# Experts' outputs summed by token in PSUM, second matrices by column halves, two more places for weights

## The chip, the core and the metric

The kernel runs on one core of a Trainium2 chip. The metric is the device time of one execution in microseconds (us); lower is better.

## The reference, cut to what matters

Two transformer blocks over 256 tokens of width 1024, all in fp32. The change is in the end of the second: a residual of cross-attention, a mixture of 32 experts with two chosen per token, and a last norm.

```python
h = rms_norm_2(x, xattn_norm_g[l])
m = rms_norm_2(mem, mem_norm_g[l])
x = x + memory_cross_attention(h, m, w_xq[l], w_xk[l], w_xv[l], w_xo[l])
h = rms_norm_2(x, moe_norm_g[l])
x = x + hierarchical_moe(h, w_group[l], b_group[l], w_router[l], b_router[l], w1[l], w3[l], w2[l])
return rms_norm_2(x, final_norm_g)

def expert_block(args):
    xb, e = args
    return (jax.nn.silu(xb @ w1[e]) * (xb @ w3[e])) @ w2[e]
```

Each expert has `w1` and `w3` of 1024x512 and `w2` of 512x1024, 2 MB each: 192 MB in all, every byte of which is read.

## The kernel before

**Layout.** The state is kept by feature: X2 is 128 partitions x 8 feature blocks x 256 tokens, the lower half of each 512-wide block of the tile X; H has the same shape. PSUM is eight banks of 128x512, handed out in turn by `banks`; `hold` takes one out of the turn.

**Experts.** They run in eight groups of four. For a group, `pe_gather` (L2481) brings up to 32 tokens an expert together with a 0/1 matrix S; `pe_up` (L2532) multiplies with `w1` and `w3`, weights moving, tokens stationary, four 32-column groups of the array at once, of which each writes its own 32 rows of a bank; `pe_turn` (L2556) transposes; `pe_down4` (L2579) multiplies with `w2`, expert j of the group in column group j; ACT copies y out of PSUM (L2590); `pe_scatter` (L2602) multiplies with the gates back to token order, and DVE adds the result to X2 (L2610). The scatter of group g - 1 stands after the up matmuls of group g. After group 7: scatter, squares by ACT (L628), their sum over partitions by 32 matmuls with ones (L2791), root, reciprocal, spreading (L611), eight gains on DVE (L663), and four DMAs of the output (L2809).

An fp32 matmul shows as two PE instructions, here called steps.

**The weights** come in units of 1 MB, two for each matrix, in the order of use: for a group first all of `w1` and `w3`, then `w2`. Before, a unit of `w2` is half of its rows; all of SP's transfers are in one written order (L2855). A unit lands in a "place", a piece of SBUF that something else has left: `FIRST_PLACES` names the first of each, and `LATER_PLACES` is then gone round in a circle; a place is free when the matmuls of its last unit are done. Most places are 2048 columns in a row; the upper or lower half of X, H or HH is 8 pieces of 256. `EXPERTS_BESIDE` names the units of the layers before behind which SP slips one expert unit each. SP issues in order and waits for each place.

```python
for n, beside in enumerate(EXPERTS_BESIDE):
    if beside == stream.units[i]:
        sp_experts(sp, n)
```

**The router** (`pe_router_steps`) takes logits, turns X2 to rows by token (L2357, HT), and keeps PE busy with nine idle matmuls (L623) while DVE chooses experts; then come the matmuls for each token's place in its expert (L2344 to L2349). If an expert has over 32 tokens, a branch (`overflowing`) computes the rest; the profiled execution does not enter it.

Of the kernel before, what the change touches and what calls it, by code (L numbers as in the profile page):

```python
# [8 lines left out]
F32 = mybir.dt.float32  # L9
# [3 lines left out]
ALU = mybir.AluOpType  # L13
# [3 lines left out]
P = 128  # L17
# [287 lines left out]
def expert_order():  # L305
    units = []
    for g in range(8):
# [7 lines left out]
                  ("w_xq_2", 0, 5), ("w_xq_2", 0, 6), ("w_xq_2", 0, 7), ("w_xo_2", 0, 5), ("w_xo_2", 0, 5), ("w_xo_2", 0, 6)]  # L315
OVER_AFTER = 3
FIRST_PLACES = ["H upper", "X upper", "ahead0", "ahead1", "con", "area1", "area2", "area3", "HH upper", "area0", "area6", "area4",
                "area5", "PPT", "YF", "ring0", "ring1", "HH lower", "his", "ring2", "side"]
LATER_PLACES = [n for n in FIRST_PLACES if n[:2] != "HH" and n[-5:] != "upper"] + ["HH0", "HH1"]
OVER_ORDER = [(name, f) for f in range(4) for name in ("w1_2", "w3_2")] + [("w2_2", k) for k in range(4)]  # L320


def two_blocks_kernel(nc, T):
    ctx = ExitStack()
    with ctx:
# [84 lines left out]
        H2 = H[:, :, 0:N]  # L410
# [16 lines left out]
        Y = [H[:, 4 * i:4 * i + 4, 256:512] for i in range(2)]  # L427
        A = [tmp[2][:, P * i:P * i + P] for i in range(2)]
# [44 lines left out]
        places = {"H upper": H[:, :, 256:512], "X upper": X[:, :, 256:512], "HH upper": hh3[:, :, 256:512], "HH lower": hh3[:, :, 0:256],  # L473
# [9 lines left out]
        over_at = next(i for i in range(24 * (OVER_AFTER + 1), len(experts.units)) if len(experts.place(i).shape) == 2)  # L483
# [1761 lines left out]
        def pe_memory(pe):  # L2245
# [12 lines left out]
            pe_open(pe, "moe")  # L2258
# [10 lines left out]
            pe_sum_last(pe, "moe", N)  # L2269

        def ac_memory(ac):
# [8 lines left out]
            for j in range(9):  # L2280
                if j < 8:
                    ac_split(ac, two_on(unit("w_xo_2", 0, 8 * j)))
                if j:
# [3 lines left out]
                    if j < 8:  # L2287
                        ac_router_gain(ac, j - 1)
# [38 lines left out]
        def ac_router_gain(ac, j):  # L2327
            ac.eng.activation(H2[:, j, :], X2[:, j, :], ACT.Identity, scale=vv("moe_norm", j)).then_inc(*ac_router.up("gain", j))

        def pe_router_steps(pe):  # L2330
# [8 lines left out]
            pe_idle(pe, "place", 9)  # L2339
# [9 lines left out]
            pe.eng.matmul(out[:, 0:32], ones[:, :], MM[:, 1, :], start=False, stop=True).then_inc(*pe_router.up("total"))  # L2349

        def pe_to_rows(pe, tb):
            for half in range(2):
                out = banks.take((ac_router, ("rows", tb, half)), "rows2", tb, half)
                pe.wait_ge(*banks.emptied("rows2", tb, half))
                for k in range(4):
                    pe.wait_ge(*ac_router.at("gain", 4 * half + k))
                    ins = pe.eng.transpose(out[:, k * P:(k + 1) * P], H2[:, 4 * half + k, tb * P:(tb + 1) * P], ident)  # L2357
# [146 lines left out]
        def ac_gates(ac, g):  # L2504
            ac.wait_ge(*pe_experts.at("back", g))
            if g >= 2:
                ac.wait_ge(*pe_experts.at("scatter", g - 2, 3))
# [644 lines left out]
```

## Time and profile before

| | us |
|---|---|
| device time, median of 3 runs | 2053.53 |
| the three runs | 2050.16 to 2053.59 |
| span of the profiled execution, first to last instruction | 2054.6 |
| PE busy in it | 1878.7 |
| PE weight loads busy | 1548.1 |
| DVE busy | 1156.9 |
| ACT busy | 903.2 |

The profile lists no time of its own for that execution beside its span. Busy times are over the whole program, of which the experts are the last quarter, so they tell little on the stage that changes. The page, the stretches and the chain are read for that stage alone. A row's "us" is the busy time of the group of instructions it stands for, and in brackets stands how long its engine had been idle and what ended that. "PEclk" is the granted TensorE clock as a share of 2.4 GHz; a single instruction is at 1.2 or at 2.4 GHz.

### The profile page before, as it was taken

Reading aid. Unit: us, or ns where it says so; the run is one execution under the profiler, and the core shown is the slowest. Engines: PE = TensorE matmul, PEld = TensorE weight load, DVE = VectorE, ACT = ScalarE, POOL = GpSimd, SP = SyncE. Lnnn points to the kernel's source line nnn. Section 1 sums busy time; section 2 is a strip of 40 time slices with the busy share of each in tenths; the row PEclk is TensorE's granted clock in tenths of the full one; section 3 lists DMA queues with packets and bytes.
Section 4 is the critical chain, followed back from the end, with each engine's and each line's share of the span. In section 5 each row is a group of like instructions: output and inputs, shape, how many; then the busy total and the mean of one; then the engine's idle time right before and its main releaser. Section 6 shows DMA issues by size and latency. Waiting matters only on the chain.

```text
span 2054.6 us, 33773 instructions
## 1 busy us (share of the span) xinstructions
PE 1878.7 (91%) x14150; PEld 1548.1 (75%) x14150; DVE 1156.9 (56%) x1910; ACT 903.2 (44%) x1532; POOL 16.9 (1%) x31
## 2 busy tenths in 40 slices
PE   7999989999999999999999999999999877767666
PEld 4877668888778888889699999997798644454434
DVE  3554767775887788568666667779765111111012
ACT  4333445664766668455455555744845100000001
POOL 0000000000000000000000000000000000000000
PEclk9999999999999999999999999999999988898898
DMA  8222014552555555225056455555275999999995
GB/s 318 91 72 82 1 72 151 184 182 97 184 177 182 194 189 189 84 99 169 1 174 212 160 184 186 185 200 191 72 252 212 411 420 420 419 419 420 421 420 235
DMA packets 93553, 427.95 MB, mean 208 GB/s; under 512 B 10065, under 2 KB 15698, under 8 KB 68946
## 3 DMA queue, kind: packets, MB, share of 16 engines
q1 hardware_dynamic: 81298, 382.45, 49.8%
q10 hardware_dynamic: 12096, 43.26, 6.3%
q8 instruction: 114, 1.87, 0.4%
q14 instruction: 45, 0.37, 0.1%
HBM read 424.62 MB, written 1.05 MB: 207 GB/s over the span
## 4 chain that ended last, share of the span: by engine, by line
PE 65%; DMA 16%; DVE 9%; ACT 5%; issue 3%; SPq 2%; ACTq 0%; DVEq 0%; POOL 0%
PE bank L535 41%; PE bank L1682 8%; DMA area<-in_w 7%; PE bank L2532 3%; DMA HH<-in_w 3%; PE bank L550 2%; SPq L2855 2%; DMA YF<-in_w 1%; DMA ring<-in_w 1%; DMA his<-in_w 1%; DMA ahead<-in_w 1%; DVE st L1333 1%; PE bank L2579 1%; ACT PPT L1278 1%; PE bank L1261 1%
## 5 line engine op out<-in xcount | busy, mean ns | idle before, releaser
L514 DVE TENSOR_TENSOR ring_r<-ring,his_r 128x1024 fp32r<-128x1024 f32 x314 | 383.4, 1223 | 222.1 <-ACT his_r L506 220.8
L535 PE MATMUL bank<-HH_r,his_r 128*128 128x256 f32 (+1 forms) x1504 | 497.9, 331 | 1.7 <-DVE ring_r L514 1.7
L535 PE MATMUL bank<-HH_r,ring_r 128*128 128x256 f32 (+1 forms) x1504 | 490.4, 326 | 0.0
L535 PE MATMUL bank<-H_r,his_r 128*128 128x256 f32 (+1 forms) x1440 | 471.7, 328 | 0.0
L506 ACT ACTIVATE his_r<-ring 128x1024 fp32r<-128x1024 f32 x314 | 330.7, 1056 | 296.5 <-PE bank L535 263.9
L535 PEld LDWEIGHTS bank<-HH_r,his_r 128*128 128x128 f32 x1504 | 285.0, 189 | 34.0 <-issue 8.7
L535 PEld LDWEIGHTS bank<-HH_r,ring_r 128*128 128x128 f32 x1504 | 283.8, 189 | 24.8
L535 PEld LDWEIGHTS bank<-H_r,his_r 128*128 128x128 f32 x1440 | 271.7, 189 | 25.2 <-issue 1.0
L2548 DVE TENSOR_TENSOR tmp<-tmp,bank 128x128 f32<-128x128 f32 x64 | 18.4, 288 | 367.2 <-ACT tmp L2541 246.0
L535 PE MATMUL bank<-area_r,his_r 128*128 128x256 f32 (+1 forms) x480 | 148.0, 321 | 0.0
L1682 PE MATMUL bank<-VT_r,his_r 128*128 128x512 f32 (+1 forms) x352 | 118.1, 335 | 0.0
L1682 PE MATMUL bank<-VT_r,ring_r 128*128 128x512 f32 (+1 forms) x352 | 117.9, 335 | 0.0
L1682 PE MATMUL bank<-YF_r,his_r 128*128 128x512 f32 (+1 forms) x352 | 117.9, 335 | 0.0
L535 PEld LDWEIGHTS bank<-area_r,his_r 128*128 128x128 f32 x480 | 89.9, 190 | 7.0
L2532 PE MATMUL bank<-area,KF 128*32 128x128 f32 x1568 | 73.1, 309 | 21.6 <-DMA area<-in_w 21.1
L2590 ACT ACTIVATE H<-bank 128x512 f32<-128x512 f32 x16 | 9.6, 597 | 188.0 <-PE bank L2579 188.0
L784 ACT ACTIVATE side<-side 128x1024 f32<-128x1024 f32 x80 | 83.6, 1045 | 1.9 <-DVE side L776 1.9
L2532 PEld LDWEIGHTS bank<-area,KF 128*32 128x32 f32 x1568 | 59.5, 124 | 32.2 <-DMA area<-in_w 28.3
L1682 PEld LDWEIGHTS bank<-YF_r,his_r 128*128 128x128 f32 x352 | 66.7, 190 | 6.9
L1409 ACT ACTIVATE VT_r<-area 128x512 fp32r<-128x512 f32 (+1 forms) x96 | 49.9, 523 | 49.8 <-PE bank L1682 44.5
L1682 PEld LDWEIGHTS bank<-VT_r,his_r 128*128 128x128 f32 x352 | 66.1, 188 | 7.0 <-DVE YF_r L1413 0.2
L1682 PEld LDWEIGHTS bank<-VT_r,ring_r 128*128 128x128 f32 x352 | 66.1, 188 | 6.9
(430 smaller groups left out, 3403.3 us busy)
## 6 DMA issues: line engine op xcount, KB each, us to landing
area<-in_w SPq DMA_DIRECT2D x70, 1024.0 KB, 27.6
ring<-in_w_in SPq DMA_DIRECT2D x102, 512.0 KB, 3.3
ring<-in_w_gate_up SPq DMA_DIRECT2D x88, 512.0 KB, 3.3
ring<-in_w SPq DMA_DIRECT2D x30, 1024.0 KB, 27.1
ring<-in_w_down SPq DMA_DIRECT2D x44, 512.0 KB, 3.4
ahead<-in_w SPq DMA_DIRECT2D x20, 1024.0 KB, 26.4
HH<-in_w SPq DMA_DIRECT2D x20, 1024.0 KB, 27.1
KX<-in_w_mod_rows ACTq DMA_DIRECT2D x28, 512.0 KB, 3.2
```

What stands on the lines that cost most here:

```text
L506: ac.eng.activation(hi_slot(n), stream.slot(u), ACT.Copy).then_inc(*ac_hi.up(n))
L514: ve.eng.tensor_tensor(lo_slot(u), stream.slot(u), hi_slot(n).bitcast(F32), ALU.subtract).then_inc(*ve_lo.up(n))
L535: ins = pe.eng.matmul(out, a, b, start=k == 0 and m == 0, stop=end)
L550: ins = pe.eng.matmul(out, a, b, start=k + m == 0, stop=k == 7 and m == 2)
L784: ac.eng.activation(prod, prod, ACT.Copy, accum_out=MODS[l][:, j, s:s + 1]).then_inc(*ac_mod.up("sum", n, s))
L1261: ins = pe.eng.matmul(out[:, 0:256], vs(kc), c.pts[g % 2][:, kc * 256:(kc + 1) * 256], start=kc == 0, stop=kc == c.nk - 1)
L1278: ac.eng.activation(p[:, m * w:(m + 1) * w], src[:, m * w:(m + 1) * w], ACT.Exp, bias=st[:, so + m:so + m + 1], scale=c.rq(h, i + m) if c. ...
L1333: ve.eng.reduce_max(st[:, so:so + c.n], src.rearrange("p (a b) -> p a b", a=c.n), AX.X, negate=True).then_inc(*ve_soft.up("max", c.site, h ...
L1409: ac.eng.activation(hi, src, ACT.Copy).then_inc(*ac_cut.up(*key))
L1682: ins = pe.eng.matmul(banks.ap("ff", l, 4 * half + n)[:, 0:t], w, x, start=k == 0 and i == 0, stop=k == 21 and i == 2)
L2532: ins = pe.eng.matmul(out[32 * n:32 * n + 32, 0:P], HG[g % 2][:, k, 32 * j:32 * j + 32], w, start=k == 0, stop=k == 7, tile_position=(0, 3 ...
L2855: sp.eng.dma_start(place, src).then_inc(experts.arrived(i)[0], 16)
```

## The change

The residual no longer lives in X2. PE copies it by token into four PSUM banks, which are held to the end (`pe_keep_tokens`, matmuls with the identity), and `pe_scatter` adds each group's outputs to them; DVE adds nothing any more. The expert input is gathered from X2 normalised by row, without the gain; ACT puts the gain on while it copies the gathered tokens, in eight pieces. A unit of `w2` is now half of its columns with all its rows, and `pe_down4` makes one half of y from the first four units and the other from the last four. The last group has a function of its own, `pe_down_last`, in which experts come one after the other. With H2 and X2 free, there are the new places "H lower" and "X lower", and "X upper" is used again in the circle: it has 22 places, before 19. One more unit is slipped in behind `w_xo_2` unit 5. The last norm is by row: ACT squares with a sum along the row, DVE and ACT scale with the root and with the gains (`GAINS`, spread over partitions in the last group), and the output leaves in two DMAs by token. The diff, without the overflow branch and without most removed lines:

```diff
+                  ("w_xq_2", 0, 5), ("w_xq_2", 0, 6), ("w_xq_2", 0, 7), ("w_xo_2", 0, 5), ("w_xo_2", 0, 5), ("w_xo_2", 0, 5),
+                  ("w_xo_2", 0, 6)]
...
+FIRST_PLACES = ["H upper", "X upper", "ahead0", "ahead1", "con", "area1", "area2", "area3", "HH upper", "area0", "area6",
+                "H lower", "area4", "area5", "PPT", "YF", "ring0", "ring1", "HH lower", "his", "ring2", "side", "X lower"]
+LATER_PLACES = [n for n in FIRST_PLACES if n[:2] != "HH" and n != "H upper"] + ["HH0", "HH1"]
...
+        def pe_keep_tokens(pe, half):
+            for tb in range(2):
+                out = banks.hold((ve_experts, ("out", tb)), "tokens", half, tb)
+                pe.wait_ge(*banks.emptied("tokens", half, tb))
+                pe.wait_ge(*ve_out.at("w_xo_2", 7))
+                for c in range(4):
+                    ins = pe.eng.matmul(out[:, c * P:(c + 1) * P], X2[:, 4 * half + c, tb * P:(tb + 1) * P], ident, start=c == 0,
+                                        stop=False)
+                ins.then_inc(*pe_router.up("kept", half, tb))
...
-            pe_idle(pe, "place", 9)
+            pe_keep_tokens(pe, 0)
...
+            pe_keep_tokens(pe, 1)
...
+                for k in range(4):
+                    ac.eng.activation(HG[i][:, 4 * half + k, :], banks.ap("gather", g, half)[:, k * P:(k + 1) * P], ACT.Identity,
+                                      scale=vv("moe_norm", 4 * half + k)).then_inc(*ac_experts.up("gathered", g, 4 * half + k))
...
+        def pe_down_part(pe, g, half, k, j):
+            w, i = experts.block("w2_2", 4 * g + j, 16 * half + 4 * k, 4)
+            pe.wait_ge(*ve_experts.at("turned", 4 * g + j))
+            pe.wait_ge(*experts.arrived(i))
...
+            experts.spent[i] = (pe_experts, ("down", g, half))
+            return pe.eng.matmul(o, AT[j][:, 32 * k:32 * k + 32], w, start=k == 0, stop=k == 3, tile_position=(0, 32 * j))
...
+        def pe_down_bank(pe, g, half):
+            banks.take((ac_experts, ("y", g, half)), "y", g, half)
+            pe.wait_ge(*banks.emptied("y", g, half))
+
...
+            for half in range(2):
+                pe_down_bank(pe, g, half)
+                for k in range(4):
+                    for j in range(4):
+                        ins = pe_down_part(pe, g, half, k, j)
+                ins.then_inc(*pe_experts.up("down", g, half))
+
+        def pe_down_last(pe, g):
+            for half in range(2):
+                pe_down_bank(pe, g, half)
+                for j in range(4):
+                    for k in range(4):
+                        ins = pe_down_part(pe, g, half, k, j)
+                    if half and j == 0:
+                        pe_scatter(pe, g, 0)
+                ins.then_inc(*pe_experts.up("down", g, half))
+            pe_scatter(pe, g, 1)
...
+        def pe_scatter(pe, g, half):
             q = g % 2
             pe.wait_ge(*ac_experts.at("back", g))
...
+            pe.wait_ge(*ac_experts.at("y", g, half))
+            for tb in range(2):
+                pe.eng.matmul(total(tb, half).rearrange("p (a b) -> p a b", a=2), SGT[q][:, tb * P:(tb + 1) * P],
+                              Y[q][:, 2 * half:2 * half + 2, :], start=False,
+                              stop=g == 7).then_inc(*pe_experts.up("scatter", g, half, tb))
+
...
+        def ve_diagonal(ve, half):
...
+            for c in range(4):
+                ve.eng.tensor_scalar(DIAG[:, c * P:(c + 1) * P], ident, vv("final_norm", 4 * half + c), None,
+                                     ALU.mult).then_inc(*ve_experts.up("diagonal", half, c))
+
+        def pe_gain_rows(pe, half):
...
+            pe.wait_ge(*ve_experts.at("diagonal", half, 3))
+            pe.eng.matmul(out, ones[:, :], DIAG, start=True, stop=True).then_inc(*pe_experts.up("gain", half))
+
...
-                pe_down4(pe, g)
+                if g < 7:
+                    pe_down4(pe, g)
+                else:
+                    pe_down_last(pe, g)
...
                 ve_turn(ve, 4 * g + 3)
...
+        def ac_square_tokens(ac, half, tb):
+            ac.wait_ge(*pe_experts.at("scatter", 7, half, tb))
+            ac.eng.activation(KF[:, 2 + tb, :], total(tb, half), ACT.Square,
+                              accum_out=squared[:, 2 * half + tb:2 * half + tb + 1]).then_inc(*ac_experts.up("squared", half, tb))
...
+            ac_sqrt_table(ac, 0, 3)
+            ac_y(ac, 7, 0)
+            for tb in range(2):
+                ac_square_tokens(ac, 0, tb)
+            ac_y(ac, 7, 1)
+            for tb in range(2):
+                ac_square_tokens(ac, 1, tb)
+                ac.wait_ge(*ac_experts.last())
+                ac.wait_ge(*ve_experts.at("start", tb))
+                ac.eng.activation(root[:, tb:tb + 1], squared[:, 2 + tb:3 + tb], ACT.Sqrt, bias=start[:, tb:tb + 1],
+                                  scale=1.0 / 1024).then_inc(*ac_experts.up("root", tb))
+            for tb in range(2):
+                o = finished(tb, 0)
+                ac.wait_ge(*ve_experts.at("rstd", tb))
+                ac.eng.activation(o, o, ACT.Identity, scale=root[:, tb:tb + 1]).then_inc(*ac_experts.up("out", tb))
...
+            for tb in range(2):
+                ve.wait_ge(*ac_experts.at("squared", 0, tb))
+                ve.wait_ge(*ac_experts.at("gain", 0))
+                ve.eng.tensor_tensor(finished(tb, 0), total(tb, 0), GAINS[:, 0, :], ALU.mult).then_inc(*ve_experts.up("gained", tb))
...
+            for tb in range(2):
+                ve.wait_ge(*ac_experts.at("root", tb))
+                ve.eng.reciprocal(root[:, tb:tb + 1], root[:, tb:tb + 1]).then_inc(*ve_experts.up("rstd", tb))
+                ve.wait_ge(*ve_experts.last())
+                ve.wait_ge(*pe_experts.at("scatter", 7, 1, tb))
+                ve.wait_ge(*ac_experts.at("gain", 1))
+                ve.eng.scalar_tensor_tensor(finished(tb, 1), total(tb, 1), root[:, tb:tb + 1], GAINS[:, 1, :], ALU.mult,
+                                            ALU.mult).then_inc(*ve_experts.up("out", tb))
...
+            for tb in range(2):
+                sp.wait_ge(*ve_experts.at("out", tb))
+                sp.wait_ge(*ac_experts.at("out", tb))
+                sp.eng.dma_start(T["out"][tb * P:(tb + 1) * P, :], HT[:, tb, :]).then_inc(s_out, 16)
+            sp.wait_ge(s_out, 32)
...
-            elif name in ("area0", "area6"):
+            elif name in ("area0", "area6", "H lower"):
...
+            elif name == "X lower":
+                sp.wait_ge(*pe_router.at("kept", 1, 1))
...
+    a = w.reshape(e, k, P, 2, 512).transpose(0, 3, 2, 1, 4)
+    return np.ascontiguousarray(a).reshape(e, 2, P, k * 512)
```

Three places show how the change moves instructions. On PE at the second matrices of group 7, before (a bank is a half of y; `waits s_e..` is a wait for a unit of weights):

```order
L2579 MATMUL bank3<-YF,tmp3 32x512 [waits s_e6]
L2579 MATMUL bank3<-ring,tmp3 32x512 [waits s_e20]
L2579 MATMUL bank3<-ring,tmp3 32x512 [waits s_e21,ve_experts]
L2579 MATMUL bank3<-his,tmp3 32x512 [waits s_e7,ve_experts]
L2579 MATMUL bank3<-YF,tmp3 32x512
L2579 MATMUL bank3<-ring,tmp3 32x512 x2
L2579 MATMUL bank3<-his,tmp3 32x512
L2579 MATMUL bank0<-YF,tmp3 32x512
L2579 MATMUL bank0<-ring,tmp3 32x512 x2
L2579 MATMUL bank0<-his,tmp3 32x512
```

And now, for the second half of y, with the scatters (L2622):

```order
L2584 MATMUL bank7<-area,tmp3 32x512 [waits s_e20]
L2584 MATMUL bank7<-area,tmp3 32x512 x3
L2622 MATMUL bank6<-H,VX 128x512 [waits ac_experts]
L2622 MATMUL bank1<-H,VX 128x512
L2584 MATMUL bank7<-PPT,tmp3 32x512 [waits s_e7]
L2584 MATMUL bank7<-PPT,tmp3 32x512 x3
L2584 MATMUL bank7<-YF,tmp3 32x512 [waits s_e8]
L2584 MATMUL bank7<-YF,tmp3 32x512 x3
L2584 MATMUL bank7<-ring,tmp3 32x512 [waits s_e22]
L2584 MATMUL bank7<-ring,tmp3 32x512 x3
L2622 MATMUL bank3<-H,VX 128x512 [waits ac_experts]
L2622 MATMUL bank0<-H,VX 128x512
```

The four experts alternated within a bank; now all four matmuls of one expert stand together, and the scatter of the first half stands behind the second half's first expert.

On SP around the end of the layers before, where `in_w1_2`, `in_w2_2` and `in_w3_2` are expert units, before:

```order
L2971 DMA ring<-in_w_xo_2 128x1024 [waits pe_products] x6
L2855 DMA area<-in_w1_2 128x2048
L2855 DMA area<-in_w3_2 128x2048
L2971 DMA ring<-in_w_xo_2 128x1024 [waits pe_products]
...
L2855 DMA side<-in_w2_2 128x2048 [waits pe_sums]
L2855 DMA ahead0<-in_w2_2 128x2048 [waits pe_experts]
L2855 DMA ahead1<-in_w2_2 128x2048
L2855 DMA con<-in_w2_2 128x2048 [waits pe_experts]
```

And now:

```order
L3029 DMA ring<-in_w_xo_2 128x1024 [waits pe_products] x6
L2914 DMA area<-in_w1_2 128x2048
L2914 DMA area<-in_w3_2 128x2048
L2914 DMA H<-in_w3_2 128x8x256
L3029 DMA ring<-in_w_xo_2 128x1024 [waits pe_products]
...
L2914 DMA side<-in_w2_2 128x2048 [waits pe_sums]
L2914 DMA X<-in_w2_2 128x8x256 [waits pe_router]
L2914 DMA X<-in_w2_2 128x8x256 [waits pe_experts]
L2914 DMA ahead0<-in_w1_2 128x2048 [waits pe_experts]
L2914 DMA ahead1<-in_w1_2 128x2048
```

A unit into H is added behind the two into area, and two into X stand ahead of `ahead0`; the first of these waits for the router's copies, and `128x8x256` is the form of the places in pieces.

On PE in the router, from the last row transposes (L2357, now L2369) to the first gather (L2481, now L2492), before:

```order
L2357 MATMUL bank7<-con,H 128x128 x4
L623 MATMUL bank6<-ones 128x128 x9
L2344 MATMUL bank1<-his,con 128x64 [waits ve_router]
L2345 MATMUL bank1<-his,ones 128x32
L2348 MATMUL bank5<-his,ones 128x32
L2349 MATMUL bank5<-his,ones 128x32
L2481 MATMUL bank4<-VX,VT 128x128 [waits ve_router,ac_router]
L2481 MATMUL bank4<-VX,VT 128x128 x7
```

And now, with the copies of the tokens (L2337):

```order
L2337 MATMUL bank6<-con,X 128x128 x4
L2337 MATMUL bank1<-con,X 128x128 x4
L2355 MATMUL bank2<-his,con 128x64 [waits ve_router,ac_norm]
L2356 MATMUL bank2<-his,ones 128x32
L2359 MATMUL bank5<-his,ones 128x32
L2360 MATMUL bank5<-his,ones 128x32
L2337 MATMUL bank3<-con,X 128x128 [waits ac_router]
L2337 MATMUL bank3<-con,X 128x128 x3
L2337 MATMUL bank0<-con,X 128x128 [waits ac_router]
L2337 MATMUL bank0<-con,X 128x128 x3
L2492 MATMUL bank4<-VX,VT 128x128 [waits ve_router,ac_router]
L2492 MATMUL bank4<-VX,VT 128x128 x7
```

Eight copies stand where the idle matmuls were, and eight more between the place matmuls and the gather.

## Rows read from the trace of the kernel before

**Rows 1.** The page: span, and GB/s in 40 slices of 51.4 us.

```profile
span 2054.6 us, 33773 instructions
...
GB/s 318 91 72 82 1 72 151 184 182 97 184 177 182 194 189 189 84 99 169 1 174 212 160 184 186 185 200 191 72 252 212 411 420 420 419 419 420 421 420 235
```

**Rows 2.** Stretches: length, PE, PEld, DVE, ACT, POOL busy; granted clock, DMA share, GB/s.

```profile
1850.00:1900.00 50.00, 36.42 (x598) 25.60 (x598) 6.66 (x20) 3.88 (x9) 0.00 (x0) 0.86 1.01 420
2024.00:2028.00 4.00, 3.63 (x28) 1.17 (x28) 0.00 (x0) 0.00 (x0) 0.00 (x0) 1.00 0.75 313
2032.00:2036.00 4.00, 3.29 (x14) 0.57 (x16) 0.00 (x0) 0.00 (x0) 0.00 (x0) 0.50 0.09 37
```

**Rows 3.** Timeline of SP's DMA issues, 1539 to 1600: start, us.

```profile
1539.11 0.91 SPq L2855 DMA_DIRECT2D area<-in_w  x2
...
1582.62 1.03 SPq L2855 DMA_DIRECT2D ring<-in_w  x2
...
1598.32 1.92 SPq L2855 DMA_DIRECT2D ahead<-in_w  x2
```

**Rows 4.** Stretches, columns as in Rows 2: one before the stream, one in its start.

```profile
1550.00:1560.00 10.00, 10.00 (x67) 9.05 (x66) 6.01 (x13) 6.61 (x13) 0.00 (x0) 1.00 0.01 4
1599.00:1604.00 5.00, 3.92 (x125) 3.54 (x117) 0.62 (x3) 0.32 (x2) 0.00 (x0) 1.00 0.96 341
```

**Rows 5.** DMA packets in 1588 to 1592 and, below it, in 1526 to 1531.

```profile
DMA packets 1047, 1.52 MB, mean 380 GB/s; under 512 B 19, under 2 KB 982, under 8 KB 982
...
DMA packets 1249, 1.91 MB, mean 382 GB/s; under 512 B 35, under 2 KB 1048, under 8 KB 1239
```

**Rows 6.** The chain that ended last: start, us, what.

```profile
2007.06 27.02 DMA HH<-in_w
...
2034.12 5.87 PE bank L2579 x26
```

**Rows 7.** PE timeline of the last second matrices.

```profile
2021.23 0.62 PE L2579 MATMUL bank<-YF,tmp 128*32 128x512 f32 x1
2021.23 0.62 PE L2579 MATMUL bank<-ring,tmp 128*32 128x512 f32 x1
2021.68 0.59 PE L2579 MATMUL bank<-YF,tmp 128*32 128x512 f32 x1
...
2024.33 0.59 PE L2579 MATMUL bank<-his,tmp 128*32 128x512 f32 x1 [1.47 <-DMA his<-in_w]
...
2027.34 0.59 PE L2579 MATMUL bank<-his,tmp 128*32 128x512 f32 x1
```

**Rows 8.** Weight loads (PEld) after the last landing.

```profile
2034.15 0.15 PEld L2579 LDWEIGHTS bank<-ring,tmp 128*32 128x32 f32 x1
...
2034.98 0.18 PEld L2579 LDWEIGHTS bank<-ring,tmp 128*32 128x32 f32 x1
...
2035.83 0.18 PEld L2579 LDWEIGHTS bank<-HH,tmp 128*32 128x32 f32 x1 [0.66 <-issue]
```

**Rows 9.** Timeline of the tail, PE, ACT and DVE.

```profile
2039.92 3.72 PE L2602 MATMUL bank<-VX,H 128*128 128x256 f32 x16
2040.03 0.60 ACT L2590 ACTIVATE H<-bank 128x512 f32<-128x512 f32 x1 [1.65 <-PE bank L2579]
2041.09 0.69 DVE L2610 TENSOR_TENSOR X<-X,bank 128x512 f32<-128x512 f32 x1 [18.98 <-PE bank L2602]
2041.81 0.63 ACT L628 ACTIVATE side<-X 128x512 f32<-128x512 f32 x1 [1.19 <-DVE X L2610]
...
2047.19 0.26 ACT L640 ACTIVATE st<-bank,epsc 128x2 f32<-128x2 f32 x1 [1.14 <-PE bank L2791]
2047.48 0.17 DVE L651 RECIPROCAL st<-st 128x2 f32<-128x2 f32 x1 [3.12 <-ACT st L640]
...
2048.45 3.22 DVE L663 SCALAR_TENSOR_TENSOR H<-X,vec,bank 128x256 f32<-128x256 f32 x8 [0.80 <-PE bank L611]
```

**Rows 10.** PE timeline at the first gather.

```profile
1590.82 1.35 PE L2481 MATMUL bank<-VX,VT 128*128 128x128 f32 x10 [0.72 <-DVE his L2450]
```

More of the change, by code:

```diff
@@ L482, in two_blocks_kernel @@
         experts = Experts(expert_order(), places, {n: sem(f"s_e{i}") for i, n in enumerate(places)})
-        over_at = next(i for i in range(24 * (OVER_AFTER + 1), len(experts.units)) if len(experts.place(i).shape) == 2)
+        over_at, over_h = [i for i in range(24 * (OVER_AFTER + 1), len(experts.units)) if len(experts.place(i).shape) == 2][0:2]
         over = Stream([(name, e, u) for e in range(32) for name, u in OVER_ORDER], [experts.place(over_at)[:, 0:UF]], [sem("f_w")], UB)
@@ L2269, in pe_memory @@
             pe_sum_last(pe, "moe", N)
+            banks.give("sum", "moe")
         def ac_memory(ac):
@@ L2475, in pe_gather @@
             for half in range(2):
-                out = banks.take((ac_experts, ("gathered", g, half)), "gather", g, half)
+                out = banks.take((ac_experts, ("gathered", g, 4 * half + 3)), "gather", g, half)
                 pe.wait_ge(*banks.emptied("gather", g, half))
@@ L2614, in pe_moe, with ac_gain_rows @@
+        def ac_gain_rows(ac, half):
+            ac.wait_ge(*pe_experts.at("gain", half))
+            ac.eng.activation(GAINS[:, half, :], banks.ap("gain", half), ACT.Copy).then_inc(*ac_experts.up("gain", half))
         def pe_moe(pe):
-            for half in range(2):
-                banks.hold((ac_experts, ("y", 7, half)), "y", half)
+            over_banks.aps = [banks.aps[i] for i in sorted(banks.idle)]
             pe_gather(pe, 0)
@@ L2645, in ac_moe @@
                         ac_gather(ac, g + 1)
-                if g == 7:
-                    ac_sqrt_table(ac, 0, 3)
-                ac_down4(ac, g)
+                    if g == 7 and j in (1, 2):
+                        ac_gain_rows(ac, j - 1)
+                if g < 7:
+                    for half in range(2):
+                        ac_y(ac, g, half)
                 if g == OVER_AFTER:
@@ L2669, in ve_moe @@
                     ve_overflow(ve)
[L2670 to L2682 removed]
+        over_banks = Slots([b[:, :] for b in psum[0:4]])
         @contextmanager
@@ L2796, in ac_output @@
[L2796 to L2810 removed]
+        squared, start, root = st[:, 0:4], st[:, 4:6], st[:, 6:8]
```

198 lines of the change are left out of this document (71 added, 127 removed).

## The prediction

> **What bounds the kernel now.** I read the page's slices first [rows 1]: from slice 32 on the core draws 410 to 420 GB/s, against some 180 before. That is the mixture of experts: 192 units of 1 MB (1,048,576 bytes), 2.50 us each at 420 GB/s. The stretches by engine [rows 2] confirm it: all DMA engines are busy while PE works 36 of 50 us, up to 2024; then the DMA engines run dry one after the other. The chain [rows 6] ends the same way: the last unit is issued at 2007.06, lands at 2034.08, and releases PE at 2034.12. So two things set the end: when the last unit lands, T = 2034.1, and the tail behind it, 2054.6 - 2034.1 = 20.5 us. What an engine does beside the stream costs nothing as long as it gives places back in time: 27 us lie between issue and landing, so some eleven units stand in the queue.
>
> **Part 1: the stream.** The diff moves three things.
> (a) One unit is fetched earlier. Now two unit transfers follow the same `w_xo_2` unit (the x2 at 1539.11 [rows 3]); the change adds a third, into the lower half of H. There is room: in 1550 to 1560 the DMA moves 4 GB/s [rows 4]. Thus 176 units instead of 177 are left for the stream that begins at 1582.6: -2.5 us.
> (b) The stream has a hole. `ahead0` can be issued only at 1598.32, when PE is done with the first unit in it [rows 3], and in 1599 to 1604 the rate is 341 instead of 420 GB/s [rows 4]: (420 - 341) x 5 / 420 = 0.9 us. The new place "X lower" is free once PE has copied the tokens to PSUM, at about 1592, and the next, "X upper", held a unit of the very first matrix, so it is free a little before 1598. All later units wait in SP's queue behind the one for X lower; but the six issued from 1582.6 on feed the DMA for 6 x 2.5 = 15 us, to about 1598. The hole closes: -0.9 us.
> (c) Three of the places that now recur, X upper, X lower and H lower, are half of a 512-wide tile, so a unit goes there as 1,024 pieces of 1 KB instead of 8 KB rows. By the list of places 24 units of the stream more than before go so. What a piece costs is seen where single such units pass [rows 5]. In 1588 to 1592 982 small packets (1.01 MB) and 0.51 MB of others took 4 us; the others take 1.22 at 420 GB/s, which leaves 2.78, or 2.90 for a whole unit: +0.40. In 1526 to 1531 it is (1048 - 35) packets, 1.04 MB, in 5 - 0.87 / 0.42 = 2.93 us: +0.46. I take 0.40, the window in the stream itself: 24 x 0.40 = +9.6 us. The bounds are 0 (a deep queue hides it) and 0.46, or 0 to +11.0 us.
> The Trainium skill speaks against this term: "DMA: Bandwidth & Descriptors", Specifications, gives 512 bytes as the least size for line rate, so 1 KB pieces would be free, the term 0 and the sum below -11.5 us. Its section on small descriptors has a fixed 3 cycles per packet on trn2; an estimate from that, 3 in 35 of 2.5 us, is 0.21 us a unit, 5 us in all and -6.5 in the sum. In rows 5 the pieces are not free.
>
> **Part 2: PE beside the stream.** The copies of the tokens add 16 matmuls of 128x128. Half take the place of nine idle ones. The other eight stand ahead of the first gather; with two steps each, at 1.35 us for ten steps [rows 10], some 2.1 us, of which 0.7 lie in the wait ahead of the gather. The gather comes about 1.4 us later and PE gives its places back later; two more places of 2.5 us each cover that, so 0. If they did not, it would cost 1.4. Scattering costs PE the same columns as before. Four PSUM banks instead of six are left to rotate, and ACT cuts a gather into eight pieces instead of two, one expert ahead; PE has 13 of 50 us free [rows 2] to hide both. The additions to X go from DVE, which has room, and the overflow branch, also rewritten, is not entered: no row of it is in the trace. All 0.
>
> **Part 3: the tail.** Before: 5.9 us of second matrices [rows 6], then scatter, four additions, squares summed over partitions, root, spreading, eight gains, output. After, once the last unit has landed:
> - PE: that unit's four matmuls, of two steps each, in one column group. The same eight steps at 2.4 GHz took from 2024.33 to 2027.93 [rows 7]: 3.6.
> - ACT copies y: 0.7. Scatter to the reader's start: 1.2 (2039.92 to 2041.09). ACT squares: 0.63. Root 0.3, reciprocal 0.2, product 0.7 (a 512-wide DVE operation took 0.69), waits between them 0.2: 7.5 us [rows 9].
> - The second half of the tokens follows by one scatter and shares the engines: its product ends at 8.3, and ACT's second scaling at 8.7.
> - Output: before, 2.9 us lie between the last DVE result (2051.7 [rows 9]) and the end, for 256 KB. Now it is 512 KB: 0.6 for the added 256 KB at 420 GB/s, and 0.2 for the other half of the tokens just ahead of it, so 3.7.
> Tail 12.4 instead of 20.5: -8.1 us. None of these forms (squares with a sum along the row, a 512-wide scaling by row) is in the trace; each is taken from the row of its engine with the same 128x512 shape, and they could each be 0.1 us off. Bounds: -9 (the outputs overlap fully) and +2.2 (PE late, below).
>
> **Does PE keep up?** That decides the tail. `pe_down_last` runs the experts one after another where `pe_down4` interleaves them. PE is ready at 2021.2 [rows 7], when the first of eight units has long landed; they come every 2.5 us. Call p the time from one expert's start to the next one's. Eight experts and a scatter (1.75 us, 4 steps of 0.43) in the middle then end at 2021.2 + 4p + 3.5 + 1.75 + 2p + 3.5 = 2030.0 + 6p, and DMA is the bound (2037.7) only if p is at most 1.3 us. Rows show groups passing each other: ring's first step starts at 2021.23, before YF's second, which is ahead of it in the program and starts at 2021.68 [rows 7]. And ring's next load comes at 2034.98 though HH's second next, ahead of it, must wait to 2035.83 [rows 8]. So a group can hold one running and at least two waiting steps while others pass, and p is at most 5 x 0.43 = 2.15. With a deeper queue it goes to nearly nothing. I take the deep queue: PE's queue passed everything in its way in the places that I could see.
>
> **Sum**: -2.5 - 0.9 + 9.6 - 8.1 = -1.9 us on a span of 2054.6. That execution's span is 1.1 above the median, so on 2053.5: 2051.6 us. The last landing comes later and the tail shrinks; the two nearly cancel.
>
> **Rivals**
> - Small pieces are cheap (0 to 0.2 us). For it: the queue is deep, and the measured units were alone. Against it: both windows say 0.4, with the DMA engines fully busy. -1.9 - 4.8 to -1.9 - 9.6: 2042.0 to 2046.8.
> - Shallow queue, p = 2.15: end of the second matrices at 2030.0 + 12.9 = 2042.9, 5.2 later than 2037.7: +3.3, so 2056.8.
> - Program order (the other side). If the experts in `pe_down_last` pass each other by their last step only, p = 7 x 0.43 = 3.0, the matrices end at 2048.0, 10.3 later: +8.4, so 2061.9. It turns the sum positive from p = 1.6. Against it: rows 7 and 8. The Trainium skill has this rule: "TensorE: Matmul & The Clock Gate", Part 3, says matmuls start and end strictly in program order, also between tiles. By that rule the time is this rival's; the starts in rows 7 disagree with it.
> - The clock. The granted clock was 0.50 in 2032 to 2036 [rows 2], that is 1.2 GHz, after PE had idled between units, and the steps took 0.85. If one group alone does not keep it up either, eight steps cost 3.5 more and the scatters 1.7: +3.3, so 2056.8. Against it: PE has no gaps now from 2017 on, and 2024 to 2028 ran at 1.00.
>
> **How the numbers follow.** 0.2% (4.1 us) is about what a measurement can tell from no change. Forecast 0.38, with pieces of 0.30 to 0.46: 2049 to 2053, of which 0.10 is beyond -0.2% and 0.28 within. Cheap pieces 0.22, all faster. Shallow queue 0.12: 0.09 same, 0.03 slower. Program order 0.13, slower. Clock 0.10: 0.07 same, 0.03 slower. Something else 0.05: 0.02, 0.02, 0.01. Faster 0.34, same 0.46, slower 0.20. The range reaches from the cheapest pieces to program order, 2042 to 2062.
>
> **What would show it.** The rate of the stream falls from 420 to some 411 GB/s (9.6 us more for some 440), most where X and H land; at 419 and more the cheap pieces were right. The rate in 1599 to 1604 is back at 410. The last unit lands 6 us later than now, at about 2040 (-3.4 + 9.6). In the last group two experts of one half start less than 1.3 us apart where their units have landed; if not, p is to be read there. Last landing to end is 12 to 13 us. Wrong altogether would be a stream below 400 GB/s, a DMA share under 1.0 in the middle (places given back too late), or a tail of over 20 us.

## The result, and the profile after

The changed kernel takes 2055.59 us (median of 20 runs, 2053.07 to 2062.60), the kernel before, run beside it, 2053.35; the ratio is 1.0023, 95% interval 1.0015 to 1.0031: 3.1 to 6.4 us slower. Measured again later it was 1.0027 (1.0018 to 1.0037). The time lies inside the range; the sign of the forecast (-1.9 us) was wrong.

The two profiles don't show it at first sight: the span after is 2051.9 us, 2.7 less than before. Executions of one kernel differ by several us, and most of that arises ahead of the experts. So every profile is read here from one event, S, the moment at which SP issues the unit for `his` in the first round of places. S lies between 1578.5 and 1589.1 in the 14 profiles; in two profiles of the changed kernel it differs by 3.9 us and the spans by 4.2. T is the last landing of a unit. The issue of `his`, in the timelines of SP's queue, before:

```profile
1584.28 2.20 SPq L2855 DMA_DIRECT2D his<-in_w  x1
```

and after, with the two stretches of the same timeline that matter below:

```profile
1578.49 2.13 SPq L2914 DMA_DIRECT2D his<-in_w  x1
...
1586.42 6.03 SPq L2914 DMA_DIRECT2D X<-in_w  x2
1593.65 3.12 SPq L2914 DMA_DIRECT2D ahead<-in_w  x2
...
1851.80 1.81 SPq L2914 DMA_DIRECT2D X<-in_w  x1
1853.65 20.24 SPq L2914 DMA_DIRECT2D HH<-in_w  x2
...
2020.70 0.43 SPq L2914 DMA_DIRECT2D ring<-in_w  x1
```

The last unit (ring) is issued at 2020.70. The view of that tile in the last 26 us of after tells when it lands:

```profile
L2914 SPq DMA_DIRECT2D ring<-in_w x1: 432/432/432, 2020.7 to 2020.7; - x1
...
DMA to landing us min/median/max: 17.2/17.2/17.2
```

T is thus 2020.70 + 17.2 = 2037.9. With [rows 6] for before: T - S goes from 449.8 to 459.4, T to the end from 20.5 to 14.0, and S to the end from 470.3 to 473.4. That is +3.1 us: the ratio's sign, and a size at the lower end of its interval. The last landing is 9.6 us later; the tail gives back 6.5.

The stretches of after (columns as in rows 2) show a stream at 409 GB/s instead of 420 [rows 2]. The hole of [rows 4] stands at S + 14.7 to 19.7, which is 1593.2 to 1598.2 here: the DMA engines are busy all the time now (share 1.06, before 0.96), but the rate is only 355 GB/s, not the 410 of the forecast, before 341. The end stays full for longer: from 9.9 to 5.9 us ahead of T the rate is 414, where before it had fallen to 313 ten us ahead of T.

```profile
1593.21:1598.21 5.00, 4.22 (x136) 3.58 (x129) 0.58 (x2) 0.66 (x2) 0.00 (x0) 1.00 1.06 355
1850.00:1900.00 50.00, 36.90 (x588) 25.58 (x588) 4.11 (x16) 4.37 (x14) 0.00 (x0) 0.86 1.03 409
2028.00:2032.00 4.00, 4.00 (x20) 1.30 (x17) 0.00 (x0) 0.00 (x0) 0.00 (x0) 1.00 0.99 414
2032.00:2036.00 4.00, 4.00 (x11) 1.01 (x8) 0.03 (x1) 1.28 (x3) 0.00 (x0) 1.00 0.47 197
```

The chain that ended last no longer ends with a transfer and a short tail [rows 6]: from 2016.2 on no landing of weights stands in it, and nearly all of it is PE (L2584 is the second matrices, L2622 the scatter, L2614 the copy of y).

```profile
1996.87 19.32 DMA area<-in_w
...
2023.26 10.89 PE bank L2584 x40
2034.16 1.92 PE bank L2622 x4
2036.07 7.06 PE bank L2584 x24
...
2043.15 0.61 ACT H L2614
2043.80 1.14 PE bank L2622 x2
```

The matrices end at 2043.13, 5.2 us after the last landing, and the end comes 8.8 us after that. PE's timeline after says why; the three experts of the second half are PPT, YF and ring:

```profile
2036.00 2.33 PE L2584 MATMUL bank<-PPT,tmp 128*32 128x512 f32 x5
2037.75 0.62 PE L2584 MATMUL bank<-YF,tmp 128*32 128x512 f32 x1
2038.17 0.59 PE L2584 MATMUL bank<-PPT,tmp 128*32 128x512 f32 x1
...
2039.49 0.62 PE L2584 MATMUL bank<-ring,tmp 128*32 128x512 f32 x1
```

All three had landed when their turn came (PPT at 2032.9, YF at 2035.4, ring at 2037.9), yet they start 1.75 and 1.74 us apart. The p of the prediction is 1.74 us: four steps of 0.43.

### The profile page after: what moved, and what is told of

It is laid out like the page before. It is cut to its first block, busy times and chain, and to the rows that moved or that the text cites. A ratio compares the mean times of both kernels' runs of the same rounds, so it can differ in the third digit from the quotient of the medians.

```text
span 2051.9 us, 33655 instructions
## 1 busy us (share of the span) xinstructions
PE 1875.7 (91%) x14064; PEld 1529.7 (75%) x14064; DVE 1133.9 (55%) x1877; ACT 911.3 (44%) x1581; POOL 16.9 (1%) x31
## 2 busy tenths in 40 slices
DMA packets 115153, 427.95 MB, mean 209 GB/s; under 512 B 10033, under 2 KB 40242, under 8 KB 93746
## 3 DMA queue, kind: packets, MB, share of 16 engines
q1 hardware_dynamic: 102898, 382.45, 51.4%
HBM read 424.62 MB, written 1.05 MB: 207 GB/s over the span
## 4 chain that ended last, share of the span: by engine, by line
PE 65%; DMA 13%; DVE 8%; ACT 6%; SPq 5%; issue 3%; ACTq 0%; DVEq 0%
PE bank L537 40%; PE bank L1684 8%; DMA area<-in_w 5%; DMA side<-in_w 5%; SPq L2914 4%; PE bank L2543 3%; PE bank L2584 2%; PE bank L552 2%; DVE st L1335 1%; ACT PPT L1280 1%; PE bank L2181 1%; DVE ring_r L516 1%; PE bank L1263 1%; PE bank L1003 1%; DMA his<-in_w 1%
## 5 line engine op out<-in xcount | busy, mean ns | idle before, releaser
L2614 ACT ACTIVATE H<-bank 128x512 f32<-128x512 f32 x16 | 9.6, 598 | 188.7 <-PE bank L2584 188.7
L2543 PE MATMUL bank<-area,KF 128*32 128x128 f32 x1216 | 70.2, 310 | 25.0 <-DMA area<-in_w 15.2
L2584 PE MATMUL bank<-area,tmp 128*32 128x512 f32 x200 | 59.0, 726 | 18.8 <-DMA area<-in_w 18.8
## 6 DMA issues: line engine op xcount, KB each, us to landing
area<-in_w SPq DMA_DIRECT2D x63, 1024.0 KB, 17.2
```

What stands on the lines that cost most here:

```text
L2543: ins = pe.eng.matmul(out[32 * n:32 * n + 32, 0:P], HG[g % 2][:, k, 32 * j:32 * j + 32], w, start=k == 0, stop=k == 7, tile_position=(0, 3 ...
L2584: return pe.eng.matmul(o, AT[j][:, 32 * k:32 * k + 32], w, start=k == 0, stop=k == 3, tile_position=(0, 32 * j))
```

## The experiments

All are read by T - S and T to the end, and by the ratio of all runs to runs of the kernel before taken beside them. Every kernel but the changed one has one profile.

**The last group side by side** (on the changed kernel)

```
 def pe_down_last(pe, g):
     for half in range(2):
         pe_down_bank(pe, g, half)
-        for j in range(4):
-            for k in range(4):
+        for k in range(4):
+            for j in range(4):
                 ins = pe_down_part(pe, g, half, k, j)
-            if half and j == 0:
-                pe_scatter(pe, g, 0)
         ins.then_inc(*pe_experts.up("down", g, half))
-    pe_scatter(pe, g, 1)
+        pe_scatter(pe, g, half)
```

> The changed kernel, with one edit: in the last group of experts the second matrices of a half run again with the four experts side by side (loop over the block outside, over the experts inside), as in groups 0 to 6, and the scatter of the first half stands between the halves. Theory A (the last group is bound by TensorE since one expert's matmuls start only 1.74 us after those of the one before): the second half's 16 matmuls take 8 steps of 0.43 us = 3.5 us after the last landing, the end comes 3.5 + 8.8 = 12.3 us after it; the last landing itself stays where it is, near 2034 in a profile that spans 2052, so about 5 us less than the changed kernel, ratio to before about 1.000. Rival B (the order costs nothing, the second half of the group is late because the experts before it end late, at 2019): the end stays 17 to 18 us after the last landing, ratio 1.002. Rival C (TensorE now waits for landings and the granted clock falls to 0.50 as it did in before's last 20 us): each step 0.85 us, so 7 us after the landing, and the scatter and the rest of the tail slower too: a gain of 0 to 2 us.

Measured: 1.0019 (1.0010 to 1.0028). T - S is 459.4, as in the changed kernel; T to the end is 12.5 instead of 14.0. The chain:

```profile
2029.45 17.17 DMA ring<-in_w
2046.62 0.04 issue
2046.67 3.63 PE bank L2584 x26
2050.30 0.02 issue
2050.32 0.61 ACT H L2612
```

3.63 us of matmuls are left behind the last landing, at full clock, and DMA is the bound again. The ratio can't tell this run from the changed kernel (1.0023); the profile does, by 1.5 us. The mechanism of theory A holds; its 5 us don't, since they rested on a last landing at 2034 in the changed kernel, where it is 2037.9. PE was only 1.5 us behind the landings. Rival C falls (eight steps in 3.63 us), rival B too.

**No places in pieces**, and both edits

```
-LATER_PLACES = [n for n in FIRST_PLACES if n[:2] != "HH" and n != "H upper"] + ["HH0", "HH1"]
+LATER_PLACES = [n.replace("H lower", "H0") for n in FIRST_PLACES if n[:2] not in ("HH", "X ") and n != "H upper"]
+LATER_PLACES += ["HH0", "HH1", "X0", "X1"]
...
-        Y = [H[:, 4 * i:4 * i + 4, 256:512] for i in range(2)]
+        Y = [H[:, 4 + 2 * i:6 + 2 * i, :].rearrange("p a (b t) -> p (a b) t", b=2) for i in range(2)]
...
+        for i in range(2):
+            places[f"X{i}"] = X[:, 4 * i:4 * i + 4, :].rearrange("p k t -> p (k t)")
+        places["H0"] = H[:, 0:4, :].rearrange("p k t -> p (k t)")
```

> The changed kernel with the same 22 places in the circle, but none of them in 1 KB pieces: the two halves of X are cut by blocks (X0, X1, each 8 KB in one piece per partition), H gives its first four blocks (H0) and the experts' outputs stand in its last four. Of the 192 units 6 stay in pieces instead of 30. Theory A (each unit in pieces costs 0.33 to 0.40 us of the stream, and the stream's end sets the end): 24 x 0.33 to 0.40 = 8 to 9.6 us less than the changed kernel, mean rate from 1600 on back at 418 to 420 GB/s, landings about 27 us; but the group of second matrices at the end stays bound by TensorE, and so its end moves with the last landing or a little less: 5 to 9.6 us less than the changed kernel, ratio to before 0.998 to 1.000. Rival B (the pieces lower the mean rate, but the 16 DMA engines then finish together, and without them the slowest engine ends where the stream with pieces does): the rate goes back to 420 and falls away in the last 10 us, the last landing stays, under 1.5 us of difference to the changed kernel, ratio 1.002.

> Both edits at once, the last group's experts side by side and no place of the circle in pieces. Theory A: the two gains add, 5 + (8 to 9.6) = 13 to 15 us less than the changed kernel, ratio to before about 0.994 to 0.996. Rival (each gain is the other's cover, one bound behind the other): only the larger of the two shows, 5 to 9 us less, ratio 0.998 to 1.000. If the pieces cost nothing at the end: 5 us less.

Measured: flat places 0.9975 (0.9964 to 0.9986), both 0.9959 (0.9945 to 0.9973). The edit takes 23 units out of pieces and not 24, as X lower as a first place stays: the page of the changed kernel counts 115,153 packets, that of the flat places 94,545, and a unit of 1,024 pieces has 896 packets more than one of 128 rows. T - S is 448.2 and 448.1: the 23 units in pieces had made it 11.3 us longer, 0.49 us each. T to the end is 14.2 and 12.5. Stretches of the run with flat places:

```profile
1800.00:1900.00 100.00, 68.24 (x1178) 48.67 (x1179) 7.79 (x31) 8.74 (x28) 0.00 (x0) 0.90 1.01 420
2024.00:2028.00 4.00, 4.00 (x20) 1.35 (x18) 0.00 (x0) 0.00 (x0) 0.00 (x0) 1.00 0.95 395
2028.00:2032.00 4.00, 4.00 (x16) 1.27 (x13) 0.00 (x0) 0.60 (x1) 0.00 (x0) 1.00 0.60 252
2032.00:2036.00 4.00, 4.00 (x10) 1.04 (x8) 0.47 (x1) 1.01 (x3) 0.00 (x0) 1.00 0.41 170
```

Rival B of the first is right in a small part: without pieces the rate is back at 420 and does fall away at the end. With what was left to move at S + 430, 420 GB/s would have ended at S + 454.9 in the changed kernel and at S + 442.6 with flat places; T comes 4.5 and 5.6 us after that (estimates from the bytes of the SP queue), so the uneven end gives back 1.1 us. The gains of both edits add: from S to the end the flat places gain 11.0 us, side by side 1.5, both 12.8; by the ratios, 0.9959 against 1.0023, it is 13. That this is theory A's 13 to 15 is luck in part: its 5 us for side by side were 1.5, and its 8 to 9.6 for the pieces 11.

**The price of a piece by itself.** Kernel before; only the shape of the two HH places of the circle changes, 18 units of the stream.

```
-LATER_PLACES = [n for n in FIRST_PLACES if n[:2] != "HH" and n[-5:] != "upper"] + ["HH0", "HH1"]
+LATER_PLACES = [n for n in FIRST_PLACES if n[:2] != "HH" and n[-5:] != "upper"] + ["HH upper", "HH lower"]
```

and for 2 KB (512 bytes with k=16 and 128 columns):

```
+        hhp = hh_flat[:, :].rearrange("p (k t) -> p k t", k=4)
+        places["HHa"], places["HHb"] = hhp[:, :, 512:1024], hhp[:, :, 0:512]
```

> The kernel before, with the two places HH0 and HH1 of the circle (each 8 KB in one piece per partition) replaced by the two halves of the same tensor cut across (HH upper, HH lower: 8 pieces of 1 KB per partition). Same places, same order, same waits; 18 more units in pieces. It measures the price of pieces by itself. Theory A: 18 x 0.33 to 0.40 = 5.9 to 7.2 us slower than before, ratio 1.0029 to 1.0035, mean rate down to about 412 GB/s. Rival B (the slowest DMA engine sets the end whatever the pieces): within 1.5 us of before, ratio 1.000, with the last landing at 2034 and the engines ending closer together.

> The kernel before, with the two HH places of the circle cut across in pieces of 2 KB (4 a partition and unit, where the run with 1 KB pieces had 8): 18 units. Theory A (a fixed cost for each piece): the 1 KB pieces cost 8.2 us by the landings (458.0 against 449.8) for 7 more pieces a partition and unit, so 3 more cost 3/7 of it: 3.5 us slower than before, ratio 1.0017. Rival B (what costs is a threshold in size, or SP's wait of 20 us behind a unit in pieces, and not the piece): either nothing, ratio 1.000, or the same 8 us, ratio 1.004.

> The same with pieces of 512 bytes, 16 a partition and unit. Theory A (a fixed cost for each piece): 15 more against 7 more, so 8.2 x 15/7 = 17.6 us slower than before, ratio 1.0086, mean rate about 399 GB/s. Rival B (the cost of the 1 KB run comes from the queue being emptied behind a unit of 1,024 pieces, SP waiting for room): with 2,048 pieces in a unit the queue holds even less, the DMA engines run dry between units (DMA share below 1.0) and the cost is more than 30 us, ratio over 1.015. The Trainium skill, DMA: Bandwidth & Descriptors, gives 512 bytes as the least size for line rate; by that rule this run would be as fast as before.

| pieces of | more pieces a partition and unit | ratio (95%) | T - S | over before |
|---|---|---|---|---|
| 8 KB (before) | 0 | 1 | 449.8 | |
| 2 KB | 3 | 1.0020 (1.0009 to 1.0031) | 453.8 | +4.0 |
| 1 KB | 7 | 1.0043 (1.0029 to 1.0057) | 457.9 | +8.1 |
| 512 bytes | 15 | 1.0079 (1.0066 to 1.0092) | 467.7 | +17.9 |

The 1 KB pieces cost more than the 5.9 to 7.2 us expected from [rows 5]; the other two came out near their 3.5 and 17.6. The end comes 20.2 to 20.5 us after T in all of them. Per unit and extra piece a partition that is 4.0/54 = 0.074, 8.1/126 = 0.064 and 17.9/270 = 0.066 us: about the same cost for each piece, and no threshold between 2 KB and 512 bytes. The Trainium skill, "DMA: Bandwidth & Descriptors", gives 512 bytes as the least size for line rate; here a 512-byte piece lowers the rate of the whole stream to 400 GB/s with one unit in ten cut so. SP's wait behind such a unit (20.24 us at 1853.65 above) is not the cause: the DMA share stays at 1.00 to 1.01 in the run with 512 bytes,

```profile
1700.00:1800.00 100.00, 71.51 (x933) 44.33 (x933) 10.88 (x30) 5.95 (x13) 0.00 (x0) 0.88 1.01 400
```

so the engines are not without work, they are slower at it.

**The changed computation with the places of before**, alone and side by side

```
-EXPERTS_BESIDE, FIRST_PLACES, LATER_PLACES of the changed kernel
+EXPERTS_BESIDE, FIRST_PLACES, LATER_PLACES of the kernel before
```

> The changed kernel's computation and order on every engine, with the places of the kernel before (21 first places, a circle of 19, no unit of H lower or X lower, 12 units beside the stream before): parts 2 and 3 of the change without part 1. Theory A (the tail is worth what its rows say): the last landing stands against the start of the circle as in before (449.8 us after his is issued), and the end comes 14 to 14.5 us after it instead of 20.5: 6 to 6.5 us less than before, ratio 0.9968 to 0.9971. Rival (the tail gives less: TensorE's last group ends later than the landings allow, or the copies of the tokens hold up the first gather and the stream): 0 to 3 us less, ratio 0.9985 to 1.000. Compared with the flat places of the run before this one, it gives what the unit fetched earlier and the three more places are worth: 1.7 us by the last landings of the two profiles, 3.4 us by the forecast.

> The changed computation with before's places, and the last group side by side: what parts 2 and 3 of the change are worth without the group's order and without the places. Theory A: last landing 451.2 us after his is issued (before: 449.8), the end 12.4 us later instead of 20.5: 6.7 us less than before by the profile, ratio 0.997 to 0.9985 (the run without side by side gave 0.9988). Rival (the tail gives less than its rows say): ratio 0.9988 or above, the end more than 14 us after the last landing.

Measured: 0.9988 (0.9979 to 0.9997) and 0.9971 (0.9960 to 0.9981). T - S is 451.1 and 450.9, T to the end 14.3 and 12.5. The first has the ratio of its rival and a last landing 1.3 us late, against theory A. The second is what theory A said: 8.0 us off the tail, 1.1 us lost before it. The first gained 2.5 us (0.6 to 4.3) by its ratio, where S to the end says 4.8 (470.3 to 465.5); whether the rest went to the time ahead of S or is chance stays open.

**The circle of 19 places**, alone and side by side. The changed kernel with `LATER_PLACES` free of H and X; the unit fetched earlier and X lower as a first place stay.

> The changed kernel, with the unit fetched earlier and all 23 first places, but a circle of the 19 places of before: H and X are used once and no more. 6 units in pieces instead of 30. Against the flat places (6 in pieces as well, circle of 22) it differs by the number of places alone. Theory A (the circle's length plays no part, since SP waits for room in the DMA queue and not for places): last landing 448 us after his is issued, as with the flat places, the end 14.3 us later, ratio 0.997 to 0.998. Rival B (with 19 places SP waits for TensorE and the queue runs lower): later by 2 to 5 us, ratio 0.999 to 1.000.

> The changed kernel with the circle of 19 places and the last group's experts side by side: all gains that the runs so far point to, in two edits. By theory A (after the last landing TensorE has 3.5 us of matmuls and 8.8 us of tail): last landing 448 us after his is issued, the end 12.5 us later, 1.8 us less than with the circle of 19 alone, ratio to before 0.995 to 0.9965. Rival (side by side brings nothing, the fall of the ratio from 0.9975 to 0.9959 with the flat places was chance): the same ratio as the circle of 19 alone, 0.9968, and the end 14.3 us after the last landing.

Measured: 0.9968 (0.9954 to 0.9982) and 0.9963 (0.9949 to 0.9976); T - S 448.0 and 447.9, T to the end 14.4 and 12.5. The three more places of the circle are worth nothing here: the same T - S as with the 22 flat ones. All that they brought was their pieces. The ratio can't tell the two runs from one another; the profiles do, by 2.0 us.

**The copies of the tokens behind the first gather** (on the run with before's places, side by side)

```
 def pe_router_steps(pe):
...
-            pe_keep_tokens(pe, 1)
...
 def pe_moe(pe):
             pe_gather(pe, 0)
+            pe_keep_tokens(pe, 1)
```

> The run before this one, with the copies of the second half of the tokens (16 matmul records, 2.03 us) moved behind the first gather. In the run with before's places the first gather started 7.80 us after his is issued, before 6.54, and the last landing came 1.4 us later than before. Theory A (the copies delay the first gather, with it the first places that come free, and with these the stream): first gather back at about 6.6, last landing at 449.8, the end 1.4 us earlier than in the run before this one (in the profile; the ratio can't tell 1.4 us). Rival (the 1.4 us are the unequal ends of the DMA engines): the first gather moves, the last landing does not.

> The changed kernel once more, unchanged, on the chip of the three others, so that their ratios can be set against it and its own profile shows how far its parts repeat. All theories: ratio to before 1.0015 to 1.0031, last landing 459.4 us after his is issued, the end 14.0 us later, the second matrices' experts of the last group 1.74 us apart.

Measured: 0.9973 (0.9962 to 0.9984), and T - S is 452.5, not 449.8. PE's timeline:

```profile
1588.17 5.44 PE L2490 MATMUL bank<-VX,VT 128*128 128x128 f32 x32 [0.72 <-DVE his L2459]
1593.44 1.95 PE L2336 MATMUL bank<-con,X 128*128 128x128 f32 x16
1595.32 0.30 PE L2541 MATMUL bank<-H,KF 128*32 128x128 f32 x2
```

and its stretch 1590 to 1592:

```profile
1590.00:1592.00 2.00, 2.00 (x12) 2.00 (x11) 0.53 (x3) 0.66 (x3) 0.00 (x0) 0.50 1.01 420
```

The gather did come earlier (S + 6.8), but the granted clock fell to 0.50 (1.2 GHz) during it, after PE had been busy for only 1.05 of the 2 us from 1586 to 1588. It took 5.44 us instead of 3.74, and the first expert began later than in the run before. The wait of 0.72 us ahead of the gather is not enough to explain this, as before has the same wait [rows 10] and its gather took 3.81 us. So the edit failed at its aim, and it still told the two theories apart: `ahead0`, which the first experts give back, is issued at S + 14.0 in before, 15.2 in the two runs with before's places (15.2 in the changed kernel too) and 17.7 here, and the last landing follows: 449.8, 451.1 and 450.9, 452.5. With before's places, a late first expert reaches the end of the stream: 1.2 us of it cost 1.1 to 1.3, 3.7 us cost 2.7.

The changed kernel once more: 1.0027 (1.0018 to 1.0037); S = 1582.42, T = 2042.1, T - S 459.7, T to the end 14.0. The parts of a profile repeat within 0.3 us though the spans (2051.9 and 2056.1) differ by 4.2.

One thing stays open. In nine of the ten measurements with the changed computation, the ratio gives 1.0 to 2.8 us more time than S to the end does (1.7 on average over the ten); in the three variants of before it is -1.4 to +0.8. The changed computation may lose that ahead of S, where nothing was read, or the one profile of before, to which all are compared, may be long by as much.

## Why the prediction was wrong

By its own steps:

- **Part 1 (c), pieces: +9.6, measured +11.3 for 23 of the 24 units.** The mechanism was right and the largest single term. The size was short: 0.40 us a unit against 0.49, above even the 0.46 from the earlier window of [rows 5]. The stream ran at 407 to 409 GB/s, not 411. The rival "small pieces are cheap" fell. By the rule of 512 bytes the sum would have been -11.5 us, not below it.
- **Part 1 (a) and (b) with Part 2: -3.4 + 0, measured -1.8** (T - S from 449.8 to between 447.9 and 448.2 without pieces in the circle; one unit in pieces is still in that). The step that failed is "The hole closes: -0.9". In the same five us after S, where before has 341 GB/s, the circle of 19 has 376 and the run with before's places 310:

```profile
1593.77:1598.77 5.00, 4.42 (x138) 3.76 (x130) 0.58 (x2) 0.66 (x2) 0.00 (x0) 1.00 1.06 376
```

```profile
1597.27:1602.27 5.00, 3.95 (x125) 3.31 (x120) 0.58 (x2) 0.66 (x2) 0.00 (x0) 1.00 0.86 310
```

With before's places the later gather opens the hole further and costs 1.1 to 1.3 us, close to the 1.4 that the prediction gave it if uncovered. With the two new places the engines stay busy (share 1.06), so the delay is covered as forecast, but only (376 - 341) x 5 / 420 = 0.4 us of the 0.9 comes back. The prediction also put the evenness of the end at nothing. From S + 430 to T the SP queue (q1) moves, in before and in the circle of 19:

```profile
q1 hardware_dynamic: 881, 6.33, 76.7%
```

```profile
q1 hardware_dynamic: 729, 5.22, 69.3%
```

At 420 GB/s these megabytes would be through at S + 445.1 and S + 442.4, 2.7 us apart; the last landings are 1.8 apart, since the DMA engines end less evenly (4.7 and 5.6 us after those moments). These are estimates from the rows shown. Why they end less evenly was not tested.

- **Part 3, tail: -8.1, measured -6.5.** The tail's own rows were right: with DMA as the bound it is 12.5 us in five kernels (12.4 forecast), and the 8.8 us behind the matrices are the 12.4 less 3.6. What failed is the step "I take the deep queue" of "Does PE keep up?". It had p near nothing; p is 1.74. Rows 7 and 8 gave the bound 5 x 0.43 = 2.15, and the truth lay nearer to that bound than to nothing: a column group's matmuls that wait hold up the following expert after four steps. By the prediction's formula p = 1.74 makes PE late by 2030.0 + 10.4 - 2037.7 = 2.7 us; it measured 1.6 (matrices end at T + 5.2 and not T + 3.6). Two moves lie between. T is 9.6 us later from S, but PE is also ready later, by 7.7 us (2023.19 here, 2021.23 in before), since the last unit of the first matrices lands later too. And PE's own chain is 0.7 us longer than the formula's. PE's readiness, which the formula has at 2021.2, in turn hangs on the clock: the last first matrices, after a wait of 1.98 us, took 3.22 us at a granted clock of 0.64 (2016 to 2020), where the run with before's places took 1.94. Before had a clock of 0.57 there too (2014.3 to 2018.3), so this moves the bound for both kernels and not the difference.

```profile
2016.23 3.22 PE L2543 MATMUL bank<-area,KF 128*32 128x128 f32 x60 [1.98 <-DMA area<-in_w]
```

- **Program order**, the rival, was wrong in its size, 3.0 for p: experts do pass each other, by four steps of eight. The rule of the Trainium skill, "TensorE: Matmul & The Clock Gate", Part 3, on strict order between tiles, is contradicted by YF's start at 2037.75, ahead of PPT's at 2038.17.
- **The clock** stayed at 1.00 from 2020 to 2048, past PE's last matmul, so the rival of a slow clock in the tail fell.

Sum: +11.3 - 1.8 - 6.5 = +3.0, the profile's 3.1, against -1.9. Three errors of 1.7, 1.6 and 1.6 us, each under 2 us and all in one direction, made the sign. The forecast was a difference of two terms near 9 us, and a chance of 0.20 for slower was too small for terms known to no better than 2 us each.

What the change gave and lost: its tail and its earlier unit are worth 5 to 7 us together by the ratios without pieces in the circle (0.9975 and 0.9968), 7.9 from S to the end, and three places in pieces take more than that. The changed kernel with the circle of 19 and the last group side by side has a ratio of 0.9963 (0.9949 to 0.9976), and with 22 flat places 0.9959 (0.9945 to 0.9973): both are faster than both kernels, and can't be told from each other.

## What to carry to other kernels

Where a stream of transfers is the bound, look at the shape of each buffer before its number: a spare half of a tile, cut across, can cost more than a place is worth, and one more place was worth nothing here, where the queue itself was full. Where the forecast is a small difference of large terms, read the profiles from a common event near the change, and compare stretches at the same distance from it, not at the same time since the start; and give the sign no more chance than the terms allow. Eight steps of one column group in a row held the next group up for four of them; side by side the four groups ran together.

## What the runs showed of the hardware

- Cutting an 8 KB row into n pieces cost 0.064 to 0.074 us for each extra piece (128 partitions, 1 MB unit), from 2 KB down to 512 bytes. In the run with 512 bytes the page counts no more packets than before, though 16 pieces a partition stand in the destination; with 1 KB it counts 16,129 more. So the time follows the pieces, and the count of packets doesn't show them all. Page rows of before, of the 1 KB and of the 512-byte run, in this order:

```profile
DMA packets 93553, 427.95 MB, mean 208 GB/s; under 512 B 10065, under 2 KB 15698, under 8 KB 68946
```

```profile
DMA packets 109682, 427.95 MB, mean 208 GB/s; under 512 B 10066, under 2 KB 34131, under 8 KB 87379
```

```profile
DMA packets 93553, 427.95 MB, mean 207 GB/s; under 512 B 10065, under 2 KB 15698, under 8 KB 68946
```

- Behind a unit of 1,024 pieces the SP queue stands for some 20 us and then issues seven units in 3 us, in after's timeline:

```profile
1829.23 19.05 SPq L2914 DMA_DIRECT2D area<-in_w  x2
1848.33 0.43 SPq L2914 DMA_DIRECT2D PPT<-in_w  x1
...
1851.32 0.43 SPq L2914 DMA_DIRECT2D side<-in_w  x1
```

With 8 KB rows it issues one about every 2.1 us. From issue to landing the last units then take 13 to 17 us instead of 27. Nothing in these runs shows a cost of that.
